# Ring slots for weight units and modulation halves, the order of halves in the mixers, the first half panel, and the last token sums

## The reference, cut to what matters

```python
for l in range(2):                                   # first block
    x = x + 0.5 * gate(0) * swiglu(norm_mod(x, 0), w_up[l, 0], w_down[l, 0])   # d_ff 2816
    x = x + gate(1) * mixer(norm_mod(x, 1), ...)     # LRU, stick-breaking and forgetting attention
    x = x + 0.5 * gate(2) * swiglu(norm_mod(x, 2), w_up[l, 1], w_down[l, 1])
for l in range(2):                                   # second block
    x = x + gt1 * (mix(h) @ w_out[l])                # pool, band, top-k and latent attention
    x = x + gt2 * ((silu(h @ w1[l]) * (h @ w3[l])) @ w2[l])
return rmsnorm(x, g_final)
```

## Time and profile before

| what | value |
|---|---|
| median of 3 runs | 1650.31 us (1643.76 to 1655.65) |
| the profiled execution, its own time | 1645.32 us |
| its span, first to last instruction | 1643.5 us |
| mean granted TensorE clock | 0.993 |
| DMA | 403 MB, 245 GB/s in the mean |

### The profile page before, as it was taken

How to read it: one execution, slowest core, us unless ns; L and a number is a source line. 1 busy time by engine, 2 the same in 40 slices (tenths; PEclk the granted TensorE clock), 3 DMA queues, 4 the chain that set the end, 5 groups by cost and what they waited for, 6 DMA issues and landing times. The chain is left out here.

```text
span 1643.5 us, 31908 instructions
## 1 busy us (share of the span) xinstructions
PE 1584.7 (96%) x13268; PEld 1562.5 (95%) x13268; DVE 1311.0 (80%) x2070; ACT 914.1 (56%) x1567; POOL 84.9 (5%) x123
## 2 busy tenths in 40 slices
PE   2999999999999999999999999999999999999998
PEld 2999998999999999998999999999999999999998
DVE  6688888788888888887788788878888878785753
ACT  5445468565545555468664545566544456564552
POOL 5000000010000000100120001001000110010000
PEclk8999999999999999999999999999999999999999
DMA  9788774358777688754378777424887863345571
GB/s 355 281 341 328 287 280 148 131 221 326 308 314 282 260 330 332 287 214 153 143 267 307 295 300 267 148 103 168 306 318 290 320 225 121 140 168 225 216 257 47
DMA packets 57136, 403.05 MB, mean 245 GB/s; under 512 B 6578, under 2 KB 6834, under 8 KB 9248
## 3 DMA queue, kind: packets, MB, share of 16 engines
q1 hardware_dynamic: 55424, 395.84, 63.4%
q0 software_dynamic: 1568, 5.17, 1.1%
HBM read 399.94 MB, written 1.05 MB: 244 GB/s over the span
## 5 line engine op out<-in xcount | busy, mean ns | idle before, releaser
L1614 DVE TENSOR_TENSOR WL<-ring,WH 128x1024 fp32r<-128x1024 f32 (+1 forms) x508 | 600.3, 1216 | 170.6 <-ACT WH L1150 169.7
L515 PE MATMUL PS<-HH,WH 128*128 128x256 f32 (+1 forms) x2640 | 632.9, 282 | 14.7 <-ACT WH L1150 9.7
L515 PE MATMUL PS<-HL,WH 128*128 128x256 f32 (+1 forms) x2640 | 622.7, 279 | 0.0
L1150 ACT ACTIVATE WH<-ring 128x1024 fp32r<-128x1024 f32 (+1 forms) x508 | 511.0, 1049 | 103.1 <-DMA ring<-in_down 45.5
L515 PEld LDWEIGHTS PS<-HH,WH 128*128 128x128 f32 x2640 | 495.2, 189 | 18.5 <-ACT WH L1150 9.9
L515 PEld LDWEIGHTS PS<-HL,WH 128*128 128x128 f32 x2640 | 493.5, 189 | 0.6
L515 PE MATMUL PS<-HH,WL 128*128 128x256 f32 (+1 forms) x2640 | 374.0, 279 | 3.7 <-DVE WL L1614 3.6
L515 PEld LDWEIGHTS PS<-HH,WL 128*128 128x128 f32 x2640 | 336.4, 189 | 5.2 <-DVE WL L1614 5.2
L1641 DVE CUSTOM_DVE_ANT_0 ring<-ring,CB,VC 128x1024 f32<-128x1024 f32 x240 | 317.6, 1338 | 10.2 <-DMA ring<-in_ada 10.1
L515 PE MATMUL PS<-AH,WL 128*128 128x256 f32 x1056 | 294.8, 279 | 0.2 <-DVE WL L1614 0.2
L515 PE MATMUL PS<-AH,WH 128*128 128x256 f32 x1056 | 294.8, 279 | 0.0
(11 more groups left out here) (210 smaller groups left out, 1438.6 us busy)
## 6 DMA issues: line engine op xcount, KB each, us to landing
ring<-in_up SPq DMA_DIRECT2D x88, 1024.0 KB, 5.9
ring<-in_ada SPq DMA_DIRECT2D x72, 1024.0 KB, 7.2
ring<-in_ffn SPq DMA_DIRECT2D x66, 1024.0 KB, 5.5
ring<-in_mod SPq DMA_DIRECT2D x48, 1024.0 KB, 6.8
ring<-in_down SPq DMA_DIRECT2D x44, 1024.0 KB, 6.3
ring<-in_win SPq DMA_DIRECT2D x32, 1024.0 KB, 7.0
ring<-in_wout SPq DMA_DIRECT2D x16, 1024.0 KB, 4.8
ring<-in_winv SPq DMA_DIRECT2D x4, 1024.0 KB, 4.8
```

The lines of the kernel that those rows point to most:

```text
L515: return e.matmul(out, lhsT, rhs, start=start, stop=stop, skip_group_check=skip)
L1150: e.activation(half_of(i)[0], slot_of(("unit", u))[:, w * (i % 2):w * (i % 2) + w], ACT.Copy).then_inc(s_hi, 1)
L1614: return e.tensor_tensor(out, a, b, op)
```

## The change

What it does, part by part:

1. **Slots.** Weight units get slots 0 to 2 of the ring for themselves (unit i in slot i % 3, loaded when unit i - 3 is used up). The modulation matrices after the first eight get slot 3, as two halves of 512 KB with a semaphore each (`s_ada`): half j of matrix i + 1 is loaded when DVE has used half j of matrix i (`s_modh`, `s_mod`).
2. **Halves elsewhere.** In `mixer1` shares 0 and 1 go ahead of `maxima(0)`, 2 and 3 behind `lo(u0 + 9)`, 4 behind `fox_tile(1)`, and 5 behind `partial(n, 1)`. `ADA_AT` follows, for both mixers; the calls in `mixer2` stay.
3. **First half panel by chunk of h.** For n > 0 PE waits for WL first and then does WH and WL with each chunk of HH as it comes.
4. **Order at the end of the mixers.** Halves 28 and 29 one chunk earlier on ACT, 28 one chunk earlier on DVE; the hi_half in `renewed` goes behind the last chunk's HH and square.
5. **Last squares.** In sub-block 9 `token_sums(c - 2)` follows each output chunk from c = 2; to free bank 2 the output chunks take banks 4, 5, 0, 1, 3, 4, 5, 3.

```diff
-ADA_AT = (9, 10, 11, 12)
+ADA_AT = {"mix1": (7, 7, 8, 8, 9, 10), "mix2": (9, 9, 10, 10, 10, 11)}
...
+        def unit_landed(i):
+            return s_slot[i % 3], 16 * (2 + i // 3 + 1)
+        def unit_at(i):
+            return ring[:, i % 3, :]
+        def ada_landed(i, j):
+            return (s_slot[i % 4], 16 * ((i + 4) % 8 // 4 + 1)) if i < FIRST_ADA else (s_ada[j], 16 * (i - FIRST_ADA + 1))
+        def ada_at(i, j):
+            return ring[:, i % 4 if i < FIRST_ADA else 3, D * j:D * j + D]
...
+        def down_bank(n, c):
+            return (4, 5, 0, 1, 2, 3, 4, 5)[c] if n + 1 < NSUB else (4, 5, 0, 1, 3, 4, 5, 3)[c]
+        def chunk_ahead(n, c):
+            return max([b for b in range(c) if down_bank(n, b) == down_bank(n, c)], default=-1)
...
+            for p in range(FIRST_ADA):
+                i = (p + 4) % 8
+                if p >= 4:
+                    e.wait_ge(s_mod, p - 3)
...
+            for i in range(3):
+                e.wait_ge(s_mod, 4 + i + 1)
+                load_unit(i)
+            e.wait_ge(s_mod, 8)
+            load_half(FIRST_ADA, 0)
+            load_half(FIRST_ADA, 1)
+            for v, (kind, i, j) in enumerate(used_up):
+                if kind == "unit":
+                    if i + 3 < len(units):
+                        e.wait_ge(s_lo, 2 * i + 2)
+                        load_unit(i + 3)
+                elif i + 1 < NADA:
+                    e.wait_ge(*((s_modh, i - FIRST_ADA + 1) if j == 0 else (s_mod, i + 1)))
...
+                    load_half(i + 1, j)
...
-                    for ks in (range(KD - 1), (KD - 1,)) if n > 0 else (range(KD),):
-                        for k in ks:
-                            e.wait_ge(s_hh, 8 * n + k + 1)
-                            mm(out, wh[:, k, :], HH[:, k, 0:S], start=k == 0, stop=False)
-                        e.wait_ge(s_lo, i + 1)
-                        for k in ks:
-                            mm(out, wl[:, k, :], HH[:, k, 0:S], start=False, stop=False)
+                    if n > 0:
+                        e.wait_ge(s_lo, i + 1)
+                    for k in range(KD):
+                        e.wait_ge(s_hh, 8 * n + k + 1)
+                        mm(out, wh[:, k, :], HH[:, k, 0:S], start=k == 0, stop=False)
+                        if n > 0:
+                            mm(out, wl[:, k, :], HH[:, k, 0:S], start=False, stop=False)
...
                         if c >= 2:
                             turned_back(c - 2)
-                        if c == 6:
-                            for b in range(5):
-                                token_sums(b)
+                            token_sums(c - 2)
                 if n == NSUB - 1:
                     turned_back(6)
-                    token_sums(5)
                     token_sums(6)
...
             def renewed(n, c):
-                if c == KD - 1:
+                if c == KD - 1 and SUBS[n][0] == "ffn":
                     hi_half(2 * (UNIT0[n + 1] + 1))
...
                 square(n + 1, c)
+                if c == KD - 1 and SUBS[n][0] != "ffn":
+                    hi_half(2 * (UNIT0[n + 1] + 1))
...
-                    if c in (3, 5):
-                        hi_half(2 * u0 + 28 + (c - 3) // 2)
+                    if c in (2, 4):
+                        hi_half(2 * u0 + 28 + (c - 2) // 2)
...
                 lo(u0 + 8)
+                share(n, 0)
+                share(n, 1)
                 maxima(0)
                 maxima(1)
                 lo(u0 + 9)
+                share(n, 2)
+                share(n, 3)
...
                 fox_tile(1)
+                share(n, 4)
                 lo(u0 + 11)
...
                 partial(n, 1)
-                share(n, 0)
+                share(n, 5)
...
-                    if c == 4:
+                    if c == 3:
                         lo_half(2 * u0 + 28)
```

More of the change, by code:

```diff
@@ L83, in ada_halves @@
     else:
-        at = [q for q in halves if ADA_AT[q // 2] == t]
+        at = [q for q in halves if ADA_AT[SUBS[n][0]][q] == t]
     return [(first + q // 2, q % 2) for q in at]
@@ L127, in build @@
         s_slot = [sem(f"s_slot{i}") for i in range(NSLOT)]
+        s_ada = [sem(f"s_ada{j}") for j in range(2)]
         s_const, s_const_rest, s_vec, s_xload = sem("s_const"), sem("s_const_rest"), sem("s_vec"), sem("s_xload")
@@ L132, in build @@
         s_hi, s_lo, s_half = sem("s_hi"), sem("s_lo"), sem("s_half")
[L134 removed]
+        s_cload, s_cb, s_mod, s_shift, s_modh = (sem("s_" + k) for k in ("cload", "cb", "mod", "shift", "modh"))
         s_astep, s_dstep = sem("s_astep"), sem("s_dstep")
@@ L209, in build @@
         UNIT0.append(len(units))
-        loads = [("ada", (i + 4) % 8) for i in range(FIRST_ADA)] + [("unit", 0)]
+        used_up = [("unit", 0, 0)]
         for n in range(NSUB):
@@ L213, in build @@
                 if UNIT0[n] + t + 1 < len(units):
-                    loads.append(("unit", UNIT0[n] + t + 1))
-                loads += [("ada", i) for i, j in ada_halves(n, t) if j == 0]
-        place = {load: p for p, load in enumerate(loads)}
+                    used_up.append(("unit", UNIT0[n] + t + 1, 0))
+                used_up += [("ada", i, j) for i, j in ada_halves(n, t)]
         def ada_source(i):
             return (f"ada{i // 36}", i % 36) if i < 72 else (f"mod{(i - 72) // 24}", (i - 72) % 24)
[L221 to L226, removed]
+        def unit_landed(i):
[6 more added lines that the diff above has]
+            return ring[:, i % 4 if i < FIRST_ADA else 3, D * j:D * j + D]
         def half_of(i):
@@ L397, in _, with load_unit, load_half @@
             spread_c(0)
[L398 to L413, removed]
+            def load_unit(i):
+                source, n = units[i]
+                e.dma_start(unit_at(i)[:, 0:2 * n], source).then_inc(s_slot[i % 3], 16)
+            def load_half(i, j):
+                name, k = ada_source(i)
+                e.dma_start(ada_at(i, j), A[name][k][:, D * j:D * j + D]).then_inc(s_ada[j], 16)
+            for p in range(FIRST_ADA):
+                i = (p + 4) % 8
+                if p >= 4:
+                    e.wait_ge(s_mod, p - 3)
+                name, k = ada_source(i)
+                e.dma_start(ring[:, p % 4, :], A[name][k]).then_inc(s_slot[p % 4], 16)
                 if p == 2:
                     e.dma_start(x_rows, A["x"].rearrange("(t p) d -> p t d", p=128)).then_inc(s_xload, 16)
-                if p == 14:
+            for i in range(3):
[11 more added lines that the diff above has]
+                    e.wait_ge(*((s_modh, i - FIRST_ADA + 1) if j == 0 else (s_mod, i + 1)))
+                    if (i, j) == (71, 1):
+                        spread_c(1)
+                    load_half(i + 1, j)
+                if v == 3:
                     e.dma_start(CN[:, 0:FIRST], A["consts"][:, 0:FIRST]).then_inc(s_const_rest, 16)
@@ L1146, in hi_half @@
                 w = units[u][1]
-                e.wait_ge(*landed(("unit", u)))
+                e.wait_ge(*unit_landed(u))
                 if i >= NSPLIT:
                     e.wait_ge(s_half, i - NSPLIT + 1)
-                e.activation(half_of(i)[0], slot_of(("unit", u))[:, w * (i % 2):w * (i % 2) + w], ACT.Copy).then_inc(s_hi, 1)
+                e.activation(half_of(i)[0], unit_at(u)[:, w * (i % 2):w * (i % 2) + w], ACT.Copy).then_inc(s_hi, 1)
             def hi(u):
@@ L1912, in mixer1 @@
                 partial(n, 3)
-                share(n, 1)
                 diagonal(n, o0 + 2)
@@ L1918, in mixer1 @@
                 tile_rest(n, o0 + 2)
-                share(n, 2)
                 partial(n, 5)
```

36 lines of the change are left out of this document (16 added, 20 removed).

## The result

The changed kernel took 1660.9 us (median of 11, 1653.9 to 1674.5) against 1649.5 us of the kernel before (median of 11, 1640.9 to 1655.7): ratio 1.0081, 95% interval 1.0053 to 1.0109. It is slower by 0.8%, where the forecast was 0.6% faster, and it lies above the range (1627 to 1657). The profiled execution has a span of 1664.1 us where the earlier trace rows has 1643.5.

The account below looks back on a forecast made before the run. The prediction took the kernel to be bound by the rate of PE's 13268 matmuls; its terms summed to -9.3 us, 1636.0 against the profiled 1645.3, forecast 1641.0 from the median 1650.3, with a range of 1627 to 1657 us.

Parts of the forecast that it names:

- The slots: Modulation loads in the ffns: separate half slots cost 0, since most halves are asked for two ticks ahead.
- The bound beside it: In the ffns: if 16 one-tick halves landed in 7.2 us, DVE waits 29 us, PE loses up to 9 us per stage.
- Rival C: In two to five ffn stages: halves come late, 9 us lost in each, 1659 to 1686 us; chance 0.06.
- The landing of a half: DMA loads: 3.2 us estimated for a half; no half in the trace lands faster than the fastest 1024 KB.
- Shares of mixer 1: Sub-blocks 1 and 4: stops behind diagonals (-1.6 us) and on X (-2.0) go; maxima come late (+2.6).
- The clock term: Behind the stop on X, 330.0 to 333.3 us: the half clock goes with the stop, -1.5 us.
- The mixers' ends: Ends of sub-blocks 1, 4, 6 and 8: PE's waits on HL fall from 6.2 to about 2 us, -4.3 us.
- First half panel: Start of ffn sub-blocks: WH and WL per chunk halve the demand for HH, -0.9 us.
- Last squares: End of sub-block 9: spreading one-column matmuls removes the half clock at 1627.1 us (-1.5), costs +0.3; net -1.2 us.
- Slots, the gain: Sub-block 9: own slots end ACT's 4.16 us stand for a weight unit, of which PE loses 0.37; -0.4 us.
- rival A: Sub-blocks 2 and 3: first panel without a stop leaves PE's slow pace, 13.6 us more, 1654.6 us; chance 0.2.
- B: Sub-blocks 5 and 7: pace falls well, to the quick one, 6.8 us less in each, 1627.4 us; chance 0.2.

Follow-up runs that it names:

- e5: The changed kernel with its four slots divided into two unit slots and two pairs of half slots: 1640.5 us, ratio 0.9938 to the kernel before.
- e1: The changed kernel without its slots (the four shared weight slots of before), the other four parts kept: 1631.4 us, ratio 0.989 to the kernel before.
- e7: The same kernel as e1, profiled once more for its paces: 1634.6 us.
- e13: The same kernel as e1, timed once more beside e14 to e16: 1631.6 us, ratio 0.992 to the kernel before.
- e16: e1 without the new places of the modulation halves in mixer 1: 1640.8 us, ratio 0.9991 to the kernel before.
- e10: The kernel before with the new last squares alone (token sums chunk by chunk, output banks changed): 1644.7 us, ratio 0.9999.
- e4: The kernel before with the new order of the first half panel alone: 1643.1 us, ratio 0.9973.
- e11: The kernel before, unchanged, profiled once more for the pace of its ffn sub-blocks: 1637.1 us.
- e9: The kernel before with the new order at the ends of the mixers alone: 1646.7 us, ratio 1.0009.
- e15: e1 without the new order at the mixers' ends: 1632.0 us, ratio 0.9922 to the kernel before.
- e8: The kernel before with the modulation shares of mixer 1 moved and nothing more: 1644.1 us, ratio 0.9984.
- e14: e1 without the new order of the first half panel: 1637.3 us, ratio 0.9972 to the kernel before.
- e12: The kernel of e6, profiled once more for its paces: 1642.8 us.
- e3: The changed kernel with modulation halves issued ahead of the tick's weight unit in the ffn sub-blocks: 1640.4 us, ratio 0.996 to the kernel before.
- e6: e1 with ScalarE's silu of the second condition row about 3.5 us earlier in sub-block 5: 1628.7 us, ratio 0.9892 to the kernel before.

## Why the prediction was wrong

*The slots.* This is the step that failed: "I take 0, because at 80% load of the DMA engines most halves are asked for two ticks ahead". Most are (180 of 222), and the 42 that aren't make 80% of the waiting. The bound beside it was nearly the truth: it had 16 halves in each ffn with one tick, 7.2 us to land, 1.8 us of waiting each. Measured are up to 14 waits in an ffn, 6.75 us, 2.4 us each. (The bound left out the 1.3 us of reading before the next load can be issued, and a quicker landing made up for part of it.) VectorE waited 29.3 us in sub-block 0, 23.6 in 2, 19.8 in 3, 13.6 in 5 and 24.1 in 7; PE's stops on WL there are 13.4, 4.7, 3.1, none and 6.4 us. Against this I had set VectorE's 20 us of idle time per stage. But PE doesn't wait for VectorE's sum over a stage, it waits for the remainders of the next unit, and a tick with two halves has next to nothing to spare: at 101.84 and 118.16 us of the kernel before VectorE goes from such a tick to the next remainders without a gap. Here the first of the two, from the tick's second reading on:

```profile
100.22 1.28 DVE L1641 CUSTOM_DVE_ANT_0 ring<-ring,CB,VC 128x1024 f32<-128x1024 f32 x1
...
101.42 0.42 DVE L1614 TENSOR_TENSOR AL<-SCR,AH 128x256 fp32r<-128x256 f32 x1
101.84 2.36 DVE L1614 TENSOR_TENSOR WL<-ring,WH 128x1024 fp32r<-128x1024 f32 x2
```

The stage totals hid it. Halves in pairs were to be seen beforehand: `ADA_N` has 42 halves for 30 ticks in sub-block 0, and slot and queue are in the diff. Rival C had the mechanism, the places and the size (1659 to 1686), and a chance of 0.06.

*The landing of a half.* From two records the prediction read that no half lands faster than the fastest 1024 KB. In the changed kernel the 224 halves take 3.1 us at the least, 6.0 in the median and 8.7 at the most, and the fastest load of 1024 KB 4.6. Its estimate of 3.2 us for a half is thus the best case and not the usual one. Nor was the size of a transfer what cost here: e5 has the same halves and no late one behind the opening.

*The clock.* The changed kernel runs at 1.2 GHz from 169.7 us for 6.8 us, and at 1145.9, 1282.4 and 1466.8 us for 3.4 us each; here the first, with the stretch after it:

```profile
169.80:176.40 6.60, 5.66 (x26) 5.67 (x27) 6.46 (x10) 4.19 (x7) 0.00 (x0) 0.50 0.81 271
176.60:183.20 6.60, 6.60 (x61) 6.60 (x60) 5.25 (x11) 3.33 (x6) 0.00 (x0) 1.00 0.88 276
```

27 weight loads against 60, the last 1 us of a stop among them. The first fall comes with PE's longest stop (excess 3.3 us, ending at 170.7), the third right after one of 2.7 us at 1281.0. Both stops are on WL, and these two falls last 10.2 us together: up to 5.1 us of loss. I had no term for falls of the clock that late halves bring. The other two come at the mixers' ends with stops of 1.31 and 0.66 us that e1 has as well, at full clock; e7, the kernel of e1 again, has a fall of 3.4 us at such a place (1129.2), and e13 has none. So these two can't be charged to the slots. All four are 17.1 us at half clock between opening and end, where the profile of before has 6.8 and e1 none: up to 8.5 us between the profiles of e1 and the change.

*Shares of mixer 1.* Right in mechanism, low in size: the stops that I named went, the price at the maxima is 1.03 us twice (taken: 2.6 in all). The terms sum to -2.5, 1.5 of it the clock behind the stop on X; e13 against e16 gives -5.9. The missing 3.4 us are mostly further stops on X and HL at the end of sub-blocks 1 and 4 (2.3 and 2.1 us less in e13), which I had put down to the mixers' ends. The clock term was less sure than it looked: of the six profiles with the stop of 2.02 us on X, two (before, e10) have the fall right behind it; e4, e11 and e16 have one only some 10 us later, e9 none.

*The mixers' ends.* -4.3 was wrong: e9 gives 0 and its interval just leaves -4.3 us out; e15 alone can't tell. The stops say it better. HL fell from 6.2 to 4.7 us in the changed kernel, not to 2, and most of that is the shares: e8, which has nothing but these, has

```profile
PEld PS L515 <- DVE HL L1617: 5.1, 7, 1.2
```

and e15 has 5.1 us too, for 4.5 in e13. In sub-blocks 6 and 8 the stops are as long as before. The row itself moves from one execution to the next: the second profile of the kernel before has 7.6 us in 10.

*First half panel.* -0.9 us; timed, it is 4 us alone (e4) and 6 us in e1 (e14), both with intervals of some 5 us on either side. No stop in the profiles explains more than 1 us. Open.

*Last squares.* The clock period at 1627 is gone in every profile with the new order, but not only there (see e10), and e10 shows no gain: 0.9999. A term of 1.2 us is below what these runs resolve.

*Slots, the gain.* ScalarE's waits for units, 68 us in the kernel before, are gone from the changed kernel's list, and PE's stop in sub-block 9 too. Only 0.4 us of that ever reached PE, as the term said.

*Pace.* I took it as unchanged and made rival A of its chance to fall badly in sub-blocks 2 and 3. There, A did not come: those two ran at 114.7 and 113.8 ns, with stops. The view behind A and B, that a stop or its absence decides it, is refuted for sub-blocks 5 and 7 by e11 and for 5 by e12. In the changed kernel's profile 5 and 7 came out quicker than in the one before (114.1 and 115.9 ns for 117.7 and 118.0), 1584 x 5.7 ns = 9 us that hide as much of the harm; 2 and 9 were 0.9 and 1.1 ns slower. That its many stops gave the pace many chances to change is a guess; it was not tried.

With the slots out, the forecast's own sum (-8.9 without their 0.4) stands against -17 and -11 us measured (e1, e13): the sign was right, the size low, and part of what was put down to the mixers' ends came with the shares.

## What to carry to other kernels

A slot that serves items in bursts must be judged by the shortest distance between two uses, not by the mean load: the wait is the time by which reading, and landing behind whatever is ahead in the queue, together exceed that distance, and the engine behind the reader pays as soon as the reader has no gap left. A shared ring in order of use (e1) gave both kinds their depth here; if slots must be separate, look first at depth (e5), then at the order of issue (e3). And take a profiled difference of 5 to 8 us in a kernel like this to the paces of its stages before giving it a cause.

## What the hardware showed that was not expected

Which of two paces a stage runs at, at full clock, is not fixed by its place in the program. In the 14 profiles of kernels with the shared ring, sub-blocks 0, 2, 3, 5 and 7 ran at 113.2 to 113.9 ns per matmul or at 117.7 to 118.0, never between in the mean of a stage, some 6.3 us apart; the same program gave either in sub-blocks 0 (e1 and e13), 5 and 7 (before and e11). Sub-block 3 was quick in all 14. What decides it is open. Between e1 and e13, one program, it is the whole difference: sub-block 0 is 5.3 us longer in e13, the span 5.2 us. 23 executions of the kernel before, in one set, spread over 1633.6 to 1663.7 us; five stages at 6.3 us each would be 31 us, but that this is where the spread comes from is not shown.

Falls of the clock differ between executions of one program too. The first profile of the kernel before has half clock at 330.0 and 1627.0 us, the second at 339.0, 1438.0 and 1619.0, for 3.4 us each.

The best kernels are those of the change without its slots: e1 at 0.989 (0.983 to 0.995) and 0.992 (0.989 to 0.995) of before in two sets, e6 at 0.989 (0.984 to 0.994) and e15 at 0.992 (0.989 to 0.995). The runs don't tell them apart.
